# Seven block products for eight in half of a down projection, over nine of eleven chunk pairs

## The reference

```python
def swiglu(x, w_gate, w_up, w_down):
    return (jax.nn.silu(x @ w_gate) * (x @ w_up)) @ w_down

h = h + swiglu(rms_norm(h, norm2_g[i]), ffn_w_gate[i], ffn_w_up[i], ffn_w_down[i])
```

## Time and profile before

| | |
|---|---|
| time, median of 3 runs | 1424.87 us (1424.51 to 1425.12) |
| profiled execution, first to last instruction (span) | 1422.4 us |
| the same execution's own time | not given apart; the runs' times lie 2.1 to 2.7 us above the span |
| PE busy | 1395.2 us |
| DVE busy | 944.7 us |
| ACT busy | 691.0 us |
| weights and other loads | 239.47 MB, mean 168 GB/s |

### The profile page before, as it was taken

The page is one execution under the profiler, slowest core; times in us unless marked ns, Lnnn a source line. Parts: engine busy times, 40 slices in busy tenths (PEclk is TensorE's granted clock), DMA queues, the critical chain, the costliest instruction groups (busy, mean ns, idle before and its releaser), DMA issues. The chain is left out here.

```text
span 1422.4 us, 25483 instructions
## 1 busy us (share of the span) xinstructions
PE 1395.2 (98%) x10044; PEld 1286.2 (90%) x10044; DVE 944.7 (66%) x1539; ACT 691.0 (49%) x1107; POOL 82.9 (6%) x137
## 2 busy tenths in 40 slices
PE   8999999999999999999999999999999999999997
PEld 8898888999989999899989999999998988899997
DVE  5778567766668666567577666676665676676665
ACT  6764545433454443376654433444433655643342
POOL 1030010000020000000000000100000123000000
PEclk9999999999999999999999999999999999999999
DMA  9344005645526555433356545365554423465540
GB/s 359 135 160 185 2 25 228 222 177 183 197 108 228 209 184 177 178 104 133 120 207 224 189 177 182 129 229 198 194 177 178 149 90 134 177 222 180 194 158 30
DMA packets 33069, 239.47 MB, mean 168 GB/s; under 512 B 6864, under 2 KB 13280, under 8 KB 14304
## 3 DMA queue, kind: packets, MB, share of 16 engines
q1 hardware_dynamic: 30320, 234.84, 45.6%
q10 hardware_dynamic: 2672, 3.58, 0.7%
HBM read 236.15 MB, written 2.25 MB: 168 GB/s over the span
## 5 line engine op out<-in xcount | busy, mean ns | idle before, releaser
L498 PE MATMUL ps<-uT_h,w_gu 128*128 128x256 f32 x3520 | 614.1, 279 | 2.5 <-ACT uT_h L1316 2.5
L498 PEld LDWEIGHTS ps<-uT_h,w_gu 128*128 128x128 f32 x3520 | 538.0, 188 | 13.8 <-issue 5.0
L498 PE MATMUL ps<-uT_l,w_gu 128*128 128x256 f32 x1760 | 478.8, 279 | 0.0
L498 PE MATMUL ps<-w_dn,h_r 128*128 128x512 f32 x1320 | 325.7, 396 | 0.3 <-DVE h_r L2070 0.3
L498 PEld LDWEIGHTS ps<-uT_l,w_gu 128*128 128x128 f32 x1760 | 325.5, 188 | 0.0
L498 PEld LDWEIGHTS ps<-w_dn,h_r 128*128 128x128 f32 x1320 | 239.6, 188 | 51.3 <-issue 1.4
L1368 ACT CAST w_gu<-ring 128x2048 fp32r<-128x2048 f32 x110 | 210.0, 1909 | 156.2 <-PE ps L498 155.6
L2028 DVE TENSOR_TENSOR w_gu<-ring,w_gu 128x2048 fp32r<-128x2048 f32 x110 | 252.1, 2292 | 35.2 <-ACT w_gu L1368 35.2
L2061 DVE TENSOR_TENSOR us<-ps,bc 128x256 f32<-128x256 f32 x110 | 46.5, 423 | 203.2 <-PE ps L498 203.2
L1381 ACT ACTIVATE wk<-wk 128x256 f32<-128x256 f32 x110 | 46.1, 419 | 260.7 <-DVE wk L2059 260.7
L1374 ACT CAST w_dn<-ring 128x1024 fp32r<-128x1024 f32 x110 | 115.7, 1052 | 82.8 <-PE ps L498 82.7
(11 more groups left out here) (398 smaller groups left out, 1696.0 us busy)
## 6 DMA issues: line engine op xcount, KB each, us to landing
ring<-wstream SPq DMA_DIRECT2D x144, 1536.0 KB, 6.6
cst<-consts_in SPq DMA_DIRECT2D x1, 2185.0 KB, 13.7
wk<-t_row ACTq DMA_DIRECT2D x1, 2048.0 KB, 8.0
wk<-masks_in SPq DMA_DIRECT2D x1, 1216.0 KB, 24.1
x<-x_in SPq DMA_DIRECT2D x2, 512.0 KB, 4.7
ring<-wstream SPq DMA_DIRECT2D x1, 1024.0 KB, 8.8
inh<-gains ACTq DMA_DIRECT2D x2, 512.0 KB, 9.6
tri_blocks<-wk SPq DMA_DIRECT2D x3, 256.0 KB, 2.8
```

Source lines behind the costliest of these rows:

```text
L498: return pe.matmul(o, l, r, start=start, stop=stop, skip_group_check=True)
```

## The change

In each block, chunks 0 to 17 form nine pairs. Of a pair's down projection (2 x 128 hidden rows by 1024 output columns, for 2 x 128 tokens), output columns 512 to 1023 are computed as before. For columns 0 to 511, taken as two blocks of 256, the product of a 2x2 block matrix (two token tiles by the pair's two chunks) with a 2x2 block matrix (two chunks by two column blocks) is made of seven block products in place of eight, each in three passes. They need sums and differences of operands: `forms` makes four of the activations (s1 to s4), `x_diff` and `y_diffs` four of the weights, each of which is then split into high and low parts. Chunks 18 to 21 keep the old scheme.

What follows from that in the program:

- the down products of a pair stand in the two steps behind it: group X (two block products, and the plain half of the even chunk) in step 2p+2, group Y (five, and the plain half of the odd chunk) in step 2p+3. Step 1 has no down products; step 19 has group Y of the last pair and chunk 18.
- two of the partial products keep PSUM banks 5 and 7 through the pairs; so gate and up results of chunks from 2 on have one bank each (4 and 6), and the gate products of a chunk wait for the eviction (`gs_ready`), the up products for the product (`h_mul`) of the chunk before.
- the up result is no longer scaled by `bc` and evicted: it is multiplied from PSUM, and the scale per token goes into `row_scale`, by which the down results are added to x. `combine`, in step 19, adds the partial products to x.
- a slot holds gate and up of chunk c and down of chunk c-2; a block has 23 slots. A slot from the third on is freed behind the Y split (`y_lo`), in twos, or behind `lo_b`.
- the high part of chunks 18 to 21's activations is copied by ScalarE, as the last piece of its step.
- the loop covers steps 6 to 17; the others are written out.

Some semaphores of other stages are merged to make room; the waits there stay the same. The core of the diff:

```diff
+        IN_X = [(0, 0, 7, 256), (2, 768, 5, 0)]
+        IN_Y = [(3, 1024, 0, 0), (5, 1792, 0, 256), (4, 2048, 2, 0), (6, 2304, 5, 256), (7, 2560, 7, 0)]
...
+            def products(p, these):
+                for i, ws, bank, lo in these:
+                    for n, (a, b) in enumerate(PASSES):
+                        last = mm(ps[bank][:, lo:lo + 256], h_r[a][:, i * P:(i + 1) * P], w_d[b][:, ws:ws + 256],
+                                  p == 0 and n == 0 and i in STARTS_BANK, p == PAIRS - 1 and n == 2)
...
                 def step(c, r=0):
-                    if 0 < c < FC - 1:
-                        pe.wait_ge(s["lo_b"], r + (q + c))
-                        pe.wait_ge(s["h_ready"], r + (q + c))
-                        down(c - 1, c == 1)
...
+                        if c > 1:
+                            pe.wait_ge(s["gs_ready"], r + (n - (c == 2)))
+                        gate_up(c, up_free)
+                    if 2 <= c < PLAIN + 2:
+                        if c % 2 == 0:
+                            pe.wait_ge(s["bx_ready"], r + (pairs + 2))
+                            pe.wait_ge(s["form_lo"], r + (pairs + 2))
+                            products(c // 2 - 1, IN_X)
+                            for t in range(TT):
+                                last = down_part(c - 2, t, 1)
+                            last.then_inc(s["dx_done"], 2)
+                        else:
+                            pe.wait_ge(s["by_ready"], r + (pairs + 2))
+                            for t in range(TT):
+                                down_part(c - 2, t, 1)
+                            products(c // 2 - 1, IN_Y).then_inc(s["dy_done"], 2)
+                    if PLAIN < c < FC:
+                        if c < FC - 1:
+                            down(f, c - 1)
...
+                        act.wait_ge(s["h_mul"], n + 1)
+                        hs = c % 2 * 3 * P
+                        act.copy(h_r[0][:, hs:hs + T], sg[:, c % 2, :]).then_inc(s["h_hi"], 1)
...
+            def forms(f, p, r=0):
+                a11, a21, s1, a12, a22, s4, s2, s3 = (form[:, k, :] for k in range(8))
+                v.wait_ge(s["h_mul"], r + (FC * f + 2 * p + 2))
+                v.tensor_tensor(s1, a21, a22, ALU.add).then_inc(s["form_ready"], 1)
+                v.tensor_tensor(s3, a11, a21, ALU.subtract).then_inc(s["form_ready"], 1)
...
+                    if c % 2 == 0 and 2 <= c <= PLAIN:
+                        y_lo(f, p - 1, r)
+                    if c % 2 and c < PLAIN:
+                        x_lo(f, p, r)
...
+                    if c % 2 and c < PLAIN:
+                        forms(f, p, r)
                     if c + 2 < FC:
                         lo_a(f, c + 2, r)
...
+                    elif c % 2:
+                        forms_lo(f, p, r)
+                        y_diffs(f, p, r)
+                    else:
+                        x_diff(f, p, r)
+                    if c == PLAIN + 1:
+                        combine(f)
```

More of the change, by code:

```diff
@@ L23 @@
 RING = 4
+PAIRS = 9
+PLAIN = 2 * PAIRS
+LOOP_FROM = 6
 NC_CMP, CMP_STRIDE = 15, 16
@@ L153, in build @@
         w_gu = over("w_gu", [P, 2, 2, 2 * D], "wk")
-        w_dn = over("w_dn", [P, 2, 2, D], "wk", 8 * D)
-        h_r = over("h_r", [P, 2, 2, T], "ffb")
+        w_d = [over(f"w_d{i}", [P, 2816], "wk", 8 * D + i * 2816) for i in range(2)]
+        h_r = [over("h_r0", [P, 8 * P], "ffb"), over("h_r1", [P, 8 * P], "inh", 2 * D)]
         ring_r = over("ring_r", [P, RING, SLOT], "ring")
@@ L549, in _, with gate_up @@
             PASSES = [(0, 0), (1, 0), (0, 1)]
-            def gate_up(j, between=None):
+            def gate_up(j, between):
                 for m in range(2):
-                    if m and between:
+                    if m:
                         between()
@@ L1287, in _, with A @@
             cnt = {}
-            def A(ins, name="a_step", n=1):
-                cnt[name] = cnt.get(name, 0) + n
+            def A(ins, name="a_step", n=1, to=None):
+                cnt[name] = to or cnt.get(name, 0) + n
                 ins.then_inc(s[name], n)
@@ L1407, in ffn @@
                     act.dma_start(scratch, t5_row).then_inc(s["t5_out"], 16)
-                step(1)
+                for c in range(1, LOOP_FROM):
+                    step(c)
                 with act.Fori(0, 4 * LOOPS, 4) as r:
                     for j in range(4):
-                        step(2 + j, r, r * 4)
-                for c in range(2 + 4 * LOOPS, FC):
+                        step(LOOP_FROM + j, r, r * 4)
+                for c in range(PLAIN, FC):
                     step(c)
@@ L1964, in _, with V @@
             cnt = {}
-            def V(ins, name="v_step"):
-                cnt[name] = cnt.get(name, 0) + 1
+            def V(ins, name="v_step", to=None):
+                cnt[name] = to or cnt.get(name, 0) + 1
                 ins.then_inc(s[name], 1)
@@ L2029, in lo_a, with b_blocks @@
                                 ALU.subtract).then_inc(s["lo_a"], 1)
-            def lo_b(f, c, r=0):
-                q, i = FC * f, BASE[f"ffn{f}"] + c
-                v.wait_ge(s["hi_b"], r + (q + c + 1))
-                v.tensor_tensor(w_dn[:, c % 2, 1, :], slot(i)[:, 2 * D:3 * D], w_dn[:, c % 2, 0, :].bitcast(F32),
+                if c < 2:
+                    v.wait_ge(s["lo_a"], q + c + 1)
+                    v.sem_inc(s[f"free{i % RING}"], 1)
+            def b_blocks(i):
+                one, two = slot(i)[:, 2 * D:3 * D], slot(i + 1)[:, 2 * D:3 * D]
+                return one[:, 0:256], one[:, 768:D], two[:, 0:256], two[:, 768:D]
@@ new lines, in y_lo @@
+            def y_lo(f, p, r=0):
+                i, n = BASE[f"ffn{f}"] + 2 * p + 2, 2 * (PAIRS * f + p)
+                v.wait_ge(s["by_hi"], r + (n + 1))
+                v.tensor_tensor(w_d[1][:, 1024:2048], slot(i + 1)[:, 2 * D:3 * D], w_d[0][:, 1024:2048].bitcast(F32),
+                                ALU.subtract)
+                v.wait_ge(s["by_hi"], r + (n + 2))
+                v.tensor_tensor(w_d[1][:, 2048:2816], diffs[:, 2048:2816], w_d[0][:, 2048:2816].bitcast(F32),
+                                ALU.subtract).then_inc(s["by_ready"], 2)
+                v.wait_ge(s["by_ready"], r + (n + 2))
+                for k in range(2):
+                    v.sem_inc(s[f"free{(i + k) % RING}"], 1)
@@ L2084, in step @@
                                         ALU.subtract).then_inc(s["small_lo"], 1)
-                    if c + 1 < FC:
-                        lo_b(f, c + 1, r)
-                lo_b(f, 0)
+                V(v.tensor_scalar(row_scale, factor, scale, None, ALU.mult))
                 v.wait_ge(s["bc_ready"], f + 1)
-                step(0)
-                step(1)
+                for c in range(2):
+                    step(c)
                 if f == 1:
```

357 lines of the change are left out of this document (246 added, 111 removed).

## The result

The changed kernel takes **1436.18 us** (median of 4 runs, 1435.73 to 1436.96) against 1424.99 for the kernel before on the same chip: the ratio is 1.0079, 95% interval 1.0065 to 1.0094. It is slower by 11.2 us, where 7.1 were forecast. The profiled execution spans 1433.9 us, 11.5 more than before.

The account below looks back on a forecast made before the run. TensorE's list of products, busy 98% of the span, bounds the kernel. Losses of 22.9 us less a gain of 15.75 make it 7.1 us slower: 1424.87 becomes 1432.0 us, range for 8 in 10 1425 to 1441.

Parts of the forecast that it names:

- the clock below 1.00 behind the wait: Sign at the block starts: TensorE's granted clock lower after its wait for chunk 2's weights would prove a rival.
- the walk: Step-by-step costing of the engines' work at starts, loop and ends: 7.1 us slower, own range 1428 to 1436, chance 0.62.
- a price of the short products above 0.1167: Sign on TensorE: a 256-column product taking more than 0.1167 us would prove the forecast gain wrong.
- gain of 45 pairs: Down products of nine pairs in five blocks: 5.25 us instead of 5.60 per pair, 15.75 us saved.
- (a): Starts of five blocks: without down products as cover TensorE waits for chunk 2's weights, 2.2 to 2.7 us each, sum 12.7.
- (b): Starts of five blocks: VectorE's 6.64 us chain to the first forms outlasts TensorE's 5.60 us of products; loss 5.2 us.
- the clock's fall: Rival, chance 0.10: TensorE drops to 1.2 GHz at each start, up to 4.6 us per block; 1455 us, or 1443.
- (c): Block 1: chunk 3's gate products wait for chunk 2's eviction, held behind the first block's scaling; loss 2.8 us.
- (d): Block ends: chunk 21's high part, behind ScalarE's next work, costs 1.0 us in blocks 0 and 2, 0.2 in 3; sum 2.2.
- The loop: Pairs in the loop: VectorE's and ScalarE's work hides, costing nothing; rival, chance 0.08: waits in every pair, 1445 us.
- the ring: Weight slots freed in twos: each lands in 6.6 us, before the conversion that reads it; costs nothing.

Follow-up runs that it names:

- the move alone: Kernel before, without block products changed: chunk 0's 12 down products moved from step 1 to step 2; 1445.56 us, ratio 1.0149.
- the short filler: Changed kernel with 20 useless 128-column products on TensorE ahead of its wait for chunk 2's weights; 1436.9 us, ratio 1.0085.
- the ends: Changed kernel with ScalarE's copy of chunk 21's high part ahead of its next conversion in each block's last step; 1435.6 us, ratio 1.0074.
- the scaling: Changed kernel with block 1's scaling of x cut into four operations, one behind each of steps 2 to 5; 1434.31 us, ratio 1.0062.
- the early split: Changed kernel with chunk 2's gate and up weights converted and split earlier, ahead of chunk 0's gate eviction; 1419.99 us, ratio 0.9964.
- the first filler: Changed kernel with 34 useless 128-column products on TensorE ahead of its wait for chunk 2's weights; 1434.58 us, ratio 1.0069.
- the three repairs: Changed kernel with chunk 2's split early, chunk 21's high part before the next conversion, block 1's scaling spread behind steps 2 to 5; 1414.02 us.

## Why the prediction was right, and where its sum was off

The direction and the mechanism held; the sum came out 4.1 us short. Of the signs that the prediction set against itself two came: the clock below 1.00 behind the wait, which came beside the walk and not in its place, and, by about 1%, a price of the short products above 0.1167. That the total was so near is in part luck: the fall, which the sum left out, takes up most of the time in which TensorE would have waited for the forms, which the sum had in. Term by term, by the positions of the groups in each block before and after:

| term | forecast | measured |
|---|---|---|
| gain of 45 pairs | -15.75 | -14.2 |
| (a) chunk 2's weights | 12.7 | 12.1 |
| (b) forms, with the clock's fall | 5.2 | 7.8 |
| (c) block 1's gate eviction | 2.8 | 2.2 |
| (d) the ends | 2.2 | 2.4 |
| elsewhere | 0 | 1.2 |
| sum | 7.1 | 11.5 (span: 11.5) |

**(a)** From a block's first gate product to chunk 2's first one it is 14.97, 15.48, 14.68, 14.69 and 14.64 us; before it was, without the 2.80 of down products and with chunk 2's 48 products at 5.60 as the prediction has them, 12.75, 13.48, 12.05, 12.03 and 12.05. The differences are 2.2, 2.0, 2.6, 2.7 and 2.6 where 2.4, 2.2, 2.7, 2.7 and 2.7 were forecast. About 0.1 us of what is missing at each start is the way from VectorE to TensorE, forecast as 0.15 and here 0.05: in block 2 the split ends at 747.45 and TensorE begins at 747.50. The walk along the chain row sums, SiLU, conversion, split was right, and the move alone shows that its cover was the down products.

**(b)** The chain of 6.64 us against 5.60 was right too: 1.09 measured in block 4, and 1.08 in block 0 with the short filler, for 1.04. What failed is the sentence that put the clock's fall among the rivals at 0.10. It took from the earlier trace rows, where no wait above 1.2 us occurs, that a fall was unlikely, although no row had a wait as long as those that (a) introduces. The fall came at four of five starts. (In three of the eleven profiles it even fell behind a wait of 0.78 us that the kernel before has as well; the rows are in the last section.) Its size was wrong as well: the rival had all 48 products, or half of them, at the lower level, 4.6 or 2.2 us a block net of the wait; it lasts 3.4 us, costs 1.5 to 1.7, and 0.6 net of the wait. In the sum the four falls are 2.4 us in (b), less 0.6 in (c).

**(c)** 2.2 in the change and 2.8 with the clock up (the X group to the Y group takes 9.93 us in the change, 10.48 with the short filler, 7.71 in block 0). The fall took 0.55 of it. **(d)** held: 1.05 and 1.04 at the ends of blocks 0 and 2, and 0.28 for 0.24 at that of block 3, whose last 24 products took 5.76 us before, 5.76 with the last chunks' high part first, and here:

```profile
1105.18 6.04 PE L516 MATMUL ps<-w_d,h_r 128*128 128x512 f32 x24
```

**The gain** was over by 1.5 us. A pair was to take 16.45 and takes 16.48. The step that failed is the unit price of 0.1167 for all products; the X group keeps it exactly, six short and six long products in 2.10 us (249.00 to 251.10), but the Y group takes 3.17 for 3.15 and each 48 gate and up products 5.60 to 5.61. The estimate by the Trainium skill (TensorE: Matmul & The Clock Gate, "Back-to-back issue gap") was 13.4 us, by a fixed part per product. The measured 14.2 is nearer to that than to 15.75; yet its mechanism isn't what the rows show, since the X group, half of it short products, has no such part.

**Elsewhere**: 0.75 us lie before block 0. They come from the kernel's first 40 products, which are the same in both kernels; first before, then now:

```profile
5.14 6.43 PE L498 MATMUL ps<-misc 128*128 128x128 f32 x40 [5.14 <-DMA cst<-consts_in]
4.98 7.27 PE L516 MATMUL ps<-misc 128*128 128x128 f32 x40 [4.98 <-DMA cst<-consts_in]
```

They took 0.21 us each at first and 0.11 later, and the quicker pace set in later here: from 8.70 to 10.30 us TensorE did 17 of them before and 10 now. In the eleven profiles block 0 begins between 225.7 and 227.2 us, and the kernel before (226.0) and the move alone made from it (227.2) lie near both ends, so this belongs to the execution and not to the change. The mixer between blocks 1 and 2 has 0.23 more, within what it varies between these profiles. The loop and the ring were costed at nothing, and cost nothing: no wait stands in any pair. Step 19 takes 11.59 us (382.99 to 394.58) for 11.55, 0.2 in five blocks.

## What to carry to other kernels

When work is taken out of a place, or moved past a synchronisation, price what it was covering before pricing the work itself: here 14 us saved over 45 pairs of chunks were lost at five places where the moved products had covered a conversion. Where a change brings in a wait of a length that the old trace doesn't contain, the old trace has nothing to say on what TensorE's clock does behind it; put it into the sum with its own price, not among the unlikely cases. And when one operand is late, find the list of the engine that makes it: here advancing work that doesn't depend on the block's scale removed the wait, while reordering what does only moved it.

## What the runs showed of the hardware

TensorE's clock fell from 1.00 to 0.50 (2.4 to 1.2 GHz) behind the waits of 2.1 to 3.2 us ahead of chunk 2 at 15 of 20 starts, in the profiles of the four kernels that have them (the change, the ends, the scaling and the move alone). In the six other experiments, where that wait is gone or under 0.7 us, it fell at 1 of 30 starts: in the early split's block 1, behind the wait of 2.5 us for the gate eviction. Four profiles have that wait with the clock up ahead of it; a fall came behind it in two (the early split and the ends) and not in the two with filler. So a wait of this length can bring a fall, and need not. The lower level lasted 3.4 us each time, and a product of 256 columns took 0.213 us in it and 0.117 outside, 1.8 times as long.

The Trainium skill (TensorE: Matmul & The Clock Gate, "HAM oscillation — how this bites in real kernels") describes a kernel whose bursts of matmuls each begin at half rate behind a wait for a DMA. These rows agree with the half rate behind a wait, at most of the starts; but the waits in the skill's example are longer than most of these, so it would not have told of a fall here.

The clock also fell in a place that no edit touches: near 193.5 us, in the mixer ahead of block 0, in three of the eleven profiles (the early split, the first filler and the three repairs). It fell behind a wait of 0.78 us that all eleven have. With the three repairs the stretch reads 0.83, with TensorE busy 9.22 of 10 us; then the products behind that wait, with the three repairs and before:

```profile
190.00:200.00 10.00, 9.22 (x67) 8.90 (x65) 7.38 (x14) 4.22 (x7) 2.48 (x2) 0.83 0.00 0
193.44 1.07 PE L1055 MATMUL ps<-cst,wk 128*128 128x128 f32 x4 [0.78 <-DVE wk L2594]
193.28 0.63 PE L989 MATMUL ps<-cst,wk 128*128 128x128 f32 x4 [0.78 <-DVE wk L2363]
```

What decides there is open; the kernel before had 1.00 in the same stretch, and TensorE just as busy. A fall there costs less than at the starts: from these products to block 0's first one it is 33.1 us in the three profiles that have it (193.44 to 226.53 with the three repairs) and 32.7 to 32.8 in the others (193.28 to 226.00 before), so 0.4 us.
